# First mixer in another order: both gate projections and both gated tiles right behind the queries and keys, then values, forget gate and attention

## What is computed

```
xn = rms_norm(h, g_mix_pre[i])
z = xn @ w_in[i]
conf_ab, q, k, v, f_logit, sc_h, sc_b, sc_c, pool_v = jnp.split(z, SPLIT_IDX, axis=-1)
y_conf = conformer_conv(conf_ab, ...)                 # u = a * sigmoid(b); 31-tap causal depthwise conv;
                                                      # layer norm, silu, @ w_conf_pw
y_att = forgetting_attention(q, k, v, f_logit + b_forget[i])   # 4 heads of 64, causal, bias from cumsum(log_sigmoid)
y_sc = short_conv_mixer(sc_h, sc_b, sc_c, w_sc[i])    # sc_b * conv3(sc_c * sc_h)
y_pool = multiscale_pool(pool_v, w_pool[i], pool_scale[i])
mix = jnp.concatenate([y_conf, y_att, y_sc, y_pool], axis=-1) @ w_out[i]
h = h + rms_norm(mix, g_mix_post[i])
```

## Time and profile before

| | us |
|---|---|
| median of 3 runs | 1515.39 (1513.42 to 1517.8) |
| the profiled execution's own time | 1511.38 |
| its span, first to last instruction | 1509.6 |
| PE busy in the span | 1455.1 (96%) |
| DVE busy | 818.1 (54%) |
| ACT busy | 571.0 (38%) |
| POOL busy | 257.7 (17%) |

### The profile page before, as it was taken

How to read it: one execution, slowest core, us unless ns; L and a number is a source line. 1 busy time by engine, 2 the same in 40 slices (tenths; PEclk the granted TensorE clock), 3 DMA queues, 4 the chain that set the end, 5 groups by cost and what they waited for, 6 DMA issues and landing times.

```text
span 1509.6 us, 17723 instructions
## 1 busy us (share of the span) xinstructions
PE 1455.1 (96%) x6972; PEld 1187.7 (79%) x6972; DVE 818.1 (54%) x1150; ACT 571.0 (38%) x836; POOL 257.7 (17%) x169
## 2 busy tenths in 40 slices
PE   7999999999999999889999999999999999999998
PEld 6776768888888887766789877788887888888887
DVE  4598566433333347674767753634444665534554
ACT  4344534522323224443364565422224443323310
POOL 4144244300101013340034202200003000000000
PEclk9999999999999999998999999999999999999999
DMA  6221222332333332211211111232332233232331
GB/s 225 70 71 56 70 71 84 98 100 96 98 98 98 98 98 74 81 56 56 71 56 52 34 56 43 89 107 86 100 106 86 70 112 103 93 111 85 98 98 70
DMA packets 35987, 129.18 MB, mean 86 GB/s; under 512 B 4008, under 2 KB 4136, under 8 KB 35904
## 3 DMA queue, kind: packets, MB, share of 16 engines
q1 hardware_dynamic: 35904, 128.04, 27.4%
HBM read 125.91 MB, written 2.10 MB: 85 GB/s over the span
## 4 chain that ended last, share of the span: by engine, by line
PE 84%; DVE 7%; ACT 3%; POOL 3%; issue 2%; DMA 0%; SPq 0%; POOLq 0%; DVEq 0%; ACTq 0%
PE P L1013 24%; PE P L1015 24%; PE P L1014 24%; PE P L1244 2%; PE P L1034 1%; PE P L1035 1%; PE P L1036 1%; DVE P L1785 1%; POOL AC L2262 1%; ACT WH L1324 1%; DVE WL L1630 1%; POOL H L2271 1%; POOL DD L2262 0%; PE P L1227 0%; PE P L1130 0%
## 5 line engine op out<-in xcount | busy, mean ns | idle before, releaser
L1013 PE MATMUL P<-AH,WH 128*128 128x512 f32 x1104 | 445.3, 403 | 25.8 <-DVE AL L1635 12.5
L1015 PE MATMUL P<-AH,WL 128*128 128x512 f32 x1104 | 433.8, 393 | 0.0
L1014 PE MATMUL P<-AL,WH 128*128 128x512 f32 x1104 | 433.6, 393 | 0.0
L1324 ACT ACTIVATE WH<-WR 128x1024 fp32r<-128x1024 f32 x233 | 245.0, 1052 | 335.1 <-PE P L1015 323.3
L1630 DVE TENSOR_TENSOR WL<-WR,WH 128x1024 fp32r<-128x1024 f32 x216 | 273.0, 1264 | 169.7 <-ACT WH L1324 169.3
L1013 PEld LDWEIGHTS P<-AH,WH 128*128 128x128 f32 x1104 | 209.6, 190 | 77.3 <-issue 27.0
L1015 PEld LDWEIGHTS P<-AH,WL 128*128 128x128 f32 x1104 | 209.4, 190 | 44.8
L1014 PEld LDWEIGHTS P<-AL,WH 128*128 128x128 f32 x1104 | 209.9, 190 | 41.9 <-issue 0.7
L1013 PE MATMUL P<-FH,WH 128*128 128x512 f32 x432 | 168.0, 389 | 0.0
L1014 PE MATMUL P<-FL,WH 128*128 128x512 f32 x432 | 168.0, 389 | 0.0
L1015 PE MATMUL P<-FH,WL 128*128 128x512 f32 x432 | 168.0, 389 | 0.0
(11 more groups left out here) (301 smaller groups left out, 1858.2 us busy)
## 6 DMA issues: line engine op xcount, KB each, us to landing
WR<-in_ws SPq DMA_DIRECT2D x233, 512.0 KB, 3.6
out<-Y SPq DMA_DIRECT2D x8, 256.0 KB, 2.0
H<-in_xT SPq DMA_DIRECT2D x3, 512.0 KB, 8.6
C<-in_const SPq DMA_DIRECT2D x1, 946.5 KB, 11.0
H<-in_xT SPq DMA_DIRECT2D x2, 256.0 KB, 4.6
PR<-in_pT SPq DMA_DIRECT2D x1, 512.0 KB, 4.5
PM<-in_params SPq DMA_DIRECT2D x1, 121.5 KB, 2.9
GKU<-in_gku SPq DMA_DIRECT2D x1, 32.0 KB, 10.5
```

What stands on the lines that cost most here:

```text
L1013: e.matmul(P, wh, xh, start=start, stop=False)
L1014: e.matmul(P, wh, xl, start=False, stop=False)
L1015: ins = e.matmul(P, wl, xh, start=False, stop=stop)
L1324: e.activation(m.WH[:, c % NW, :], m.WR[:, c % NRAW, :], ACT.Copy).then_inc(*at.up("w_hi", "w_hi", c))
```

## The change

Three edits, all in the planner. The gates and the glu tiles move ahead of the values, and with them the start of `conformer`. The start of `attention1` moves from the end of the first glu tile to the end of the first pooling tile. Part 0 takes its four inputs in the order 4, 5, 6, 7, and `values1` comes 2 ticks behind `turn1` instead of 1.

```
         for q in range(4):
             self.say("qk1", q, out[q])
             self.close(out[q])
+        for j in range(2):
+            self.say("glu_gate", j, out[4 + j])
+            self.close(out[4 + j])
+        for j in range(2):
+            t = self.tile(fm(128 * j), A)
+            self.say("glu", j, t)
+            self.close(t)
+            if j == 0:
+                self.beside(self.conformer())
         got = self.tokens("w_in", 1024, 2, "A1")
...
         self.beside(self.forget())
-        for j in range(2):
-            self.say("glu_gate", j, out[4 + j])
-            self.close(out[4 + j])
-        for j in range(2):
-            t = self.tile(fm(128 * j), A)
-            self.say("glu", j, t)
-            self.close(t)
-            if j == 0:
-                self.beside(self.conformer())
-                self.beside(self.attention1())
...
         pool(0)
+        self.beside(self.attention1())
...
-        part([6, 7, 4, 5], 0)
+        part([4, 5, 6, 7], 0)
...
-        yield 1
+        yield 2
         if h % 2 == 0 and n == 0:
             self.o1 = self.bank(7)
         self.say("values1", u, self.o1)
```

## The result

The kernel after took 1525.26 us (median of 4; 1521.87 to 1525.55) against 1514.41 us (4 runs, 1511.6 to 1517.8): ratio 1.0071, 95% interval 1.0052 to 1.009. Seven more runs in a later study gave 1522.12 against 1513.13 us, ratio 1.0051 (1.0032 to 1.0069). So the new order is 0.5 to 0.7% slower, 8 to 11 us. The forecast was +5.1 us, 1520.5, with a range of 1511 to 1526.

A forecast was written before the change was run, and what follows sets the result against it. The prediction took DVE and PE together to bound attention and convolution, DVE setting the last tap. ln_mean at 150.0 plus 65.4 gave 215.4 against 210.33, +5.1; added to 1515.4, 1520.5 us, range 1511 to 1526.

The forecast's parts named there:

- The forecast's own band: Whole program: the main case, slower by +3 to +8 us, given a chance of 0.5.
- worse by more: Rival: all DVE waits stay, the clock also falls at the first wait and lasts; +10, 1525.5 us, chance 0.13.
- Step a: Up to the first pooling tile: it starts at 74.7 instead of 78.5, gaining 3.8 us, the gate wait and its slow clock.
- slow clock: PE at 1.2 GHz after waits: 1.7 us lost behind the old gate wait, 1.4 us expected behind the new values1 wait.
- Step b: Pooling tile to last tap: DVE lags, first mask at 97.7, PE waits about 5 us, ln_mean at 150.0.
- The two forget operations: On DVE ahead of the pooling tile: 1.6 us each, or 0.75 if like others of 512 elements.
- Step c: From P = 61 (ln_mean) to part 2's end: 65.4 us instead of 54.1, with ln_out among attention's last units.
- New wait of `values1`: At unit 13, PE waits 4.1 us while ln_out, a table load, exp and a copy hold ACT.
- The wait for unit 13's mask: ln_var's sums and root steps stand ahead of the mask on DVE; scores1 of unit 14 comes about 0.4 us early.
- The small edits win nothing: Part 0's input order and later values1 lie ahead of P = 61, where DVE sets the time: no gain.
- The rival that the early start pays: DVE not behind when attention begins, first mask by 93: about 1512.5 us, chance 0.15.

The follow-up runs named there:

- e1: The kernel before with only the two glu_gate steps moved right behind qk1, ahead of the values: 1511.66 us against 1514.94, ratio 0.9985.
- e3: The kernel before with only later values1 (two ticks behind turn1) and part 0's input order 4, 5, 6, 7: 1510.4 us, ratio 0.9978.
- e2: The kernel after with values1 again one tick behind turn1 and part 0 in the order 6, 7, 4, 5: 1526.37 us, ratio 1.0088.

## Why the prediction was right

The direction and the place of each loss were right; the size, +5.1, was half to two thirds of the measured 8 to 11. The forecast's own band, +3 to +8, holds the second study's ratio (7.7 us) and misses the first (10.8) and both differences of medians (10.9 and 9.0). That 1525.26 lies inside 1511 to 1526 owes something to the width of the range: it is the size of the rival *worse by more* (1525.5, chance 0.13). One condition of that rival, the clock that falls at the first wait too, did come about. By its own steps:

- **Step a**, first pooling tile at 74.7: 74.29. From L1076 it comes at 38.4, where the prediction's 74.7 less the 36.23 of before is 38.5. The gates' step alone is worth 3.3 us by the medians (e1, at the edge of the noise). The prediction gave the wait a slow clock of 1.7 us; e3's trace has the same wait of 1.97 us without it, so this part of the 3.8 us is not there in every run.
- **Step b**, DVE late. First mask done at 97.7: 98.13. Wait about 5 us: 5.79. `ln_mean` at 150.0: 151.61, which from L1076 is 115.7 instead of 113.8, 1.9 us late; 0.7 of it was already there at the first mask. The two forget operations took 0.68 and 0.67, not 1.6, so the pooling tile was taken at 82.98 instead of 84.3; what was saved there went into the pooling mean, 2.45 us where its twin at 89.48 took 0.75 (POOL was at work beside it, see the last section).
- **Step c**, from `ln_mean` to the mixer's end 65.4 us: 218.22 - 151.61 = 66.6. New wait of `values1` 4.1 us: 4.25, with the table load of 1.28 and exp right behind it (177.87), as the row of before had it. The wait for unit 13's mask was 0.18, not 0.4.
- **What was mis-sized** is the slow clock. I took 1.4 us, once, behind `values1`. It came three times: 2.8 us of PE time behind the first mask, 1.7 behind `ln_mean`, which waited only 0.85 us, and 1.7 behind `values1`; the mixer before lost 1.7, once. It counts in full only where PE sets the time, behind `ln_mean`: 1.7 + 1.7 = 3.4 against my 1.4, 2.0 more. The stretch from `ln_mean` to the mixer's end was 66.6 against 65.4, 1.2 more, so the other terms of step c came out 0.8 too high together. With `ln_mean` itself 1.9 us late, that is the 3.1 us between 5.1 and the 8.2 that the mixer lost. The last 1 to 3 us lie in later stages, where the granted clock differs between the two traces.
- **The small edits win nothing** does not stand for the new order, as far as e2 tells. They hardly move the last tap (115.6 and 114.9 from L1076), but in the traced runs the input order keeps `ln_mean` from starting 3.3 us further behind it. I had looked at which event ends last with the edit and not at what ends last without it. In the kernel before, their gain is in the medians and not in the trace.
- **The rival that the early start pays** needed the first mask by 93; it came at 98.13. Even with 15 us less for DVE the new order stays at 1.0011 of the kernel before (0.9996 to 1.0027).

Shown by an experiment: that the gates' step removes PE's wait, and the cost of `ln_out` among the last units (two edits, both with the predicted sign). Shown in part: DVE's load as a cause. By the traces the two together come near the 8.2 to 9.4 us that the mixer lost (4.4 to 5.5 and 2.8 to 3.9), but no run has both taken away. What the three slow stretches cost together was read from traces and not taken away by itself.

## What to carry to other kernels

A chain of dependent steps that hops between in-order engines (product, silu, high part, low part) should be said when nothing urgent follows on any of them; here it cost a matmul wait of 4 us when it was moved among the last attention units, and all of that wait went with a later place, a third of it (1.4 us) with two swapped lines. Filling an engine's idle time ahead of a wait only helps if what it then meets is not already full: count that engine's work up to the next step that the bound engine needs from it. Allow for a slower clock behind every new wait of PE, short ones too. And before you compare times of two traces, look at where each of them begins.

## What was not expected of the hardware

- In the kernel after a wait of 0.85 us, followed by sixteen matmuls with one column, left a stretch at 1.2 GHz (granted 0.71 in 156 to 160), where one of 1.7 us in the kernel before had not (1.00). Even the same wait need not end the same: the 1.97 us for the gate product were followed by 0.50 (66 to 68 us) before, and by the full clock in e3, where every step up to there is the same. How long a wait is does not tell by itself whether the clock falls. Rows of e3:

```profile
64.14 0.50 PE L1013 MATMUL P<-AH,WH 128*128 128x512 f32 x1 [1.97 <-DVE SG L1762]
```

```profile
64.00:66.00 2.00, 1.86 (x8) 1.56 (x9) 1.97 (x3) 1.98 (x3) 1.64 (x2) 1.00 0.00 0
66.00:68.00 2.00, 2.00 (x11) 1.65 (x10) 0.17 (x1) 1.82 (x3) 1.83 (x2) 1.00 0.00 0
```

- The mean granted clock of a run goes with its time: before, 0.993 with 1509.9 us and 0.987 with 1516.7; after, 0.985 with 1521.9 and 0.983 with 1525.4. A difference of 0.006 is 9 us of 1510, so most of the spread of one kernel's runs, some 8 us, can be this.
- Some DVE operations on SBUF stretched beside POOL. One of 16 columns that takes 0.17 us took 2.25 in the kernel after (127.15), and the forget operation of 0.68 took 1.65 before. In these rows the DVE operation was held when POOL's had begun first, and ended soon after POOL's: at 129.40 against 129.37, and the pooling mean of 2.45 us at 89.04 against 88.50. The one at 126.39, begun 0.1 us ahead of POOL's, took only 0.73. DVE's rows and POOL's:

```profile
126.39 0.73 DVE L1831 SCALAR_TENSOR_TENSOR DD<-S,C,PV 64x512 f32<-64x512 f32 x1
127.15 2.25 DVE L1835 TENSOR_TENSOR DD<-S,C 64x16 f32<-64x16 f32 x1
129.43 0.17 DVE L1838 TENSOR_TENSOR DD<-DD,PV 64x16 f32<-64x16 f32 x1
```

```profile
86.10 2.40 POOL L2252 TENSOR_TENSOR WL<-WR,WH 128x1024 fp32r<-128x1024 f32 x1 [0.17 <-POOL S L2299]
126.50 2.87 POOL L2252 TENSOR_TENSOR WL<-WR,WH 128x1024 fp32r<-128x1024 f32 x1 [0.17 <-POOL SC L2307]
```
